# A two-layer hybrid decoder trunk on one NeuronCore: parameter rows fetched with one transfer per kind and turned one tile later, SBUF operands moved by 64 bytes, a table load and three convolution taps placed elsewhere

## What is computed

```python
def token_mixer(h, w_in, w_gate_up, b_gate, gla_norm_w, conv_w, conv_b, cn_w, cn_b, w_out):
    z = h @ w_in
    q, k, v, g, gr, ca, cb = split(z)
    gate_logit = gr @ w_gate_up + b_gate
    log_a = log_sigmoid(gate_logit) / 16
    o = rmsnorm(gla_chunked(q / 8, k, v, log_a), gla_norm_w) * silu(g)
    u = ca * sigmoid(cb)
    u = causal_dwconv(u, conv_w, conv_b)            # 31 taps, each channel by itself
    u = silu(layernorm(u, cn_w, cn_b))
    return concatenate([o, u]) @ w_out

for l in range(2):
    x = x + token_mixer(rmsnorm(x, ln1_w[l]), ...)
    h = rmsnorm(x, ln2_w[l])
    x = x + (swiglu(h, ...) if l == 0 else moe_swiglu(h, ...))
return rmsnorm(x, final_norm_w)
```

## Time and profile before

| | us |
|---|---|
| median of 3 runs | 1210.83 (1210.68 to 1210.93) |
| the profiled execution | 1211.27 |
| its span, first to last instruction | 1209.4 |
| PE busy in it | 1191.6 (99%) |
| DVE busy | 966.9 (80%) |
| ACT busy | 784.1 (65%) |

### The profile page before, as it was taken

The page is one execution under the profiler, slowest core; times in us unless marked ns, Lnnn a source line. Parts: engine busy times, 40 slices in busy tenths (PEclk is TensorE's granted clock), DMA queues, the critical chain, the costliest instruction groups (busy, mean ns, idle before and its releaser), DMA issues.

```text
span 1209.4 us, 16633 instructions
## 1 busy us (share of the span) xinstructions
PE 1191.6 (99%) x6712; PEld 1020.5 (84%) x6712; DVE 966.9 (80%) x890; ACT 784.1 (65%) x693; POOL 93.9 (8%) x160
## 2 busy tenths in 40 slices
PE   8999999999999999999999999999999999999997
PEld 7997999999899788888888888888888888888885
DVE  4988664445667879899979879879889879979987
ACT  5857644334565757677677768668668668767764
POOL 8320000000122000000000000000000000000000
PEclk9999999999999999999999999999999999999999
DMA  8982555555557259999999999999999999999980
GB/s 246 354 247 73 192 174 180 197 181 179 204 176 242 67 190 360 387 369 390 378 368 392 374 377 385 375 377 386 377 387 374 383 383 372 379 386 374 395 331 37
DMA packets 185003, 362.78 MB, mean 300 GB/s; under 512 B 10568, under 2 KB 70746, under 8 KB 184922
## 3 DMA queue, kind: packets, MB, share of 16 engines
q1 hardware_dynamic: 178170, 343.22, 79.4%
q0 software_dynamic: 6736, 18.43, 4.3%
q10 hardware_dynamic: 16, 0.00, 0.0%
HBM read 350.64 MB, written 7.86 MB: 296 GB/s over the span
## 4 chain that ended last, share of the span: by engine, by line
PE 93%; DVE 3%; ACT 1%; SPq 1%; issue 1%; DMA 0%; ACTq 0%; DVEq 0%
PE YB L2215 18%; PE WBS L2194 13%; PE WBS L2196 13%; PE WBS L2195 13%; PE YB L1804 5%; PE WBS L1731 5%; PE WBS L1733 4%; PE WBS L1732 4%; PE YB L2206 2%; PE WBS L1765 2%; PE YB L2230 2%; PE WBS L1767 2%; PE WBS L1766 2%; PE YB L1985 1%; PE YB L1785 1%; PE YB L1731 1%
## 5 line engine op out<-in xcount | busy, mean ns | idle before, releaser
L1006 DVE TENSOR_TENSOR w_lo<-raw,w_hi 128x2048 fp32r<-128x2048 f32 x319 | 716.1, 2285 | 85.8 <-ACT w_hi L611 85.6
L611 ACT ACTIVATE w_hi<-raw 128x2048 fp32r<-128x2048 f32 x324 | 598.3, 1914 | 12.8 <-DMA raw<-in_w_in 8.4
L2194 PE MATMUL WBS<-w_hi,t_hi 128*128 128x512 f32 x704 | 279.0, 396 | 0.5 <-DVE w_lo L1006 0.5
L2196 PE MATMUL WBS<-w_hi,t_lo 128*128 128x512 f32 x704 | 275.1, 391 | 0.0
L2195 PE MATMUL WBS<-w_lo,t_hi 128*128 128x512 f32 x704 | 274.2, 389 | 0.0
L2194 PEld LDWEIGHTS WBS<-w_hi,t_hi 128*128 128x128 f32 x704 | 132.2, 188 | 29.5 <-issue 2.5
L2196 PEld LDWEIGHTS WBS<-w_hi,t_lo 128*128 128x128 f32 x704 | 132.1, 188 | 28.5
L2195 PEld LDWEIGHTS WBS<-w_lo,t_hi 128*128 128x128 f32 x704 | 132.4, 188 | 26.3
L1731 PE MATMUL WBS<-t_hi,w_lo 128*128 128x256 f32 x448 | 127.5, 285 | 0.0
L1732 PE MATMUL WBS<-t_hi,w_hi 128*128 128x256 f32 x448 | 126.8, 283 | 0.0
L1733 PE MATMUL WBS<-t_lo,w_hi 128*128 128x256 f32 x448 | 126.7, 283 | 0.0
(11 more groups left out here) (320 smaller groups left out, 1390.9 us busy)
## 6 DMA issues: line engine op xcount, KB each, us to landing
raw<-in_we_down SPq DMA_DIRECT2D x88, 1024.0 KB, 7.1
raw<-in_we_gate SPq DMA_DIRECT2D x80, 1024.0 KB, 6.8
raw<-in_we_up SPq DMA_DIRECT2D x80, 1024.0 KB, 6.8
raw<-in_w_in SPq DMA_DIRECT2D x19, 1024.0 KB, 5.8
raw<-in_wd_gate SPq DMA_DIRECT2D x11, 1024.0 KB, 5.3
raw<-in_wd_up SPq DMA_DIRECT2D x11, 1024.0 KB, 5.3
raw<-in_wd_down SPq DMA_DIRECT2D x11, 1024.0 KB, 4.9
raw<-in_w_out SPq DMA_DIRECT2D x8, 1024.0 KB, 9.3
```

The costliest lines, as they stand in the source:

```text
L611: act.activation(w_hi[:, hi_slot(n, item), :], raw[slot][:], ACT.Copy).then_inc(hi_ready, 1)
L1006: dve.tensor_tensor(w_lo[slot][:], raw[slot][:], w_hi[:, hi_slot(n, item), :].bitcast(F32), ALU.subtract).then_inc(lo_ready, 1)
L2194: pe.matmul(bank, xs_hi[:, k0 + k, :], hi[:, k, :], start=start, stop=False)
L2196: ins = pe.matmul(bank, xs_lo[:, k0 + k, :], hi[:, k, :], start=False, stop=stop)
```

## The change

- **Transfers.** `small()` is called once. `conv_w`, `b_gate`, `conv_b`, `cn_w`, `cn_b` and `gla_norm_w` are each fetched for both layers with one transfer: 6 transfers in place of 12, of the same bytes in all. The rows of `pv_rows`, and so the columns of `pv`, now stand by kind and then by layer, and `param(l, at0, count, k)` gives a column's place.
- **Turning.** In layer 0 `turn_params()` follows tile 1 of V0 on PE, where it stood ahead of it. Both of its instructions wait for `rows_ready`, now for 7 transfers.
- **`ident4`.** DVE's reduction of the identity (L1219), which only the convolution weights need later, follows the copy of `gr_t`.
- **Addresses.** `idle` grows from 48 to 64 numbers. Every tile behind it moves up by 64 bytes: those that stood 64 bytes past a multiple of 128 now start on one, and a few (`shift_w`, `o_ss`, `rout`, `before`, `slot_no`) the other way round.
- **Table.** `preload(ACT.Sqrt)` stands ahead of `place(0)` in both layers.
- **Taps.** In layer 1 the last `conv(5)`, which stood ahead of `sum_groups(0)`, is cut: `conv(3)` now stands between `add_ahead(0)` and `head_sums(0)`, and `conv(2)` stays.

```diff
-        idle = sb("idle", [P, 48])
+        idle = sb("idle", [P, 64])
...
+        def param(l, at0, count, k=0):
+            return slice(L * at0 + count * l + k, L * at0 + count * l + k + 1)
...
-            def small(l):
-
-                sp.dma_start(tap_rows[2 * TAPS * l:2 * TAPS * (l + 1), :], conv_w[l, :, 0:2 * P].rearrange("w (c p) -> w c p", p=P)).then_inc(rows_ready, 16)
+            def small():
+
+                sp.dma_start(tap_rows[0:2 * TAPS * L, :], conv_w[:, :, 0:2 * P].rearrange("l w (c p) -> (l w) c p", p=P)).then_inc(rows_ready, 16)
                 for src, at0, k in ((b_gate, PV_BG, KT), (conv_b, PV_CB, CT), (cn_w, PV_CW, CT), (cn_b, PV_CBB, CT), (gla_norm_w, PV_GN, 1)):
-                    r = l * NPV + at0
-                    sp.dma_start(pv_rows[r:r + k, :], src[l].rearrange("(c p) -> c p", p=P)).then_inc(rows_ready, 16)
+                    sp.dma_start(pv_rows[L * at0:L * (at0 + k), :], src.rearrange("l (c p) -> (l c) p", p=P)).then_inc(rows_ready, 16)
...
-                        for layer in range(L):
-                            small(layer)
+                        small()
...
                     gates()
+                    preload(ACT.Sqrt)
                     place(0)
-                    preload(ACT.Sqrt)
                     head_squares()
...
                     dve.tensor_copy(taps[:].rearrange("p l w c -> p (l w c)"), YB[:, 2, 0:pv_at])
-                    dve.tensor_reduce(ident4[:], ident[:].rearrange("p (s j) -> p j s", s=4), AX, ALU.add).then_inc(ident4_ready, 1)
...
                 dve.tensor_copy(gr_t, YB[0:2 * RANK, 0, 0:T]).then_inc(gr_copied, 1)
+                if l == 0:
+                    dve.tensor_reduce(ident4[:], ident[:].rearrange("p (s j) -> p j s", s=4), AX, ALU.add).then_inc(ident4_ready, 1)
...
                     add_ahead(0)
+                    conv(3)
                     head_sums(0)
                     head_sums(1)
                     head_gates()
                     add_ahead(1)
                     head_lo(0)
                     head_lo(1)
-                    conv(5)
+                    conv(2)
                     sum_groups(0)
...
                 if l == 0:
+                    tokens_tile("V0", 1)
                     turn_params()
-                    tokens_tile("V0", 1)
...
-                pe.wait_ge(rows_ready, 16 * (6 * L + 1))
+                pe.wait_ge(rows_ready, 16 * 7)
```

More of the change, by code:

```diff
@@ L138, in trunk @@
         NPV = KT + 3 * CT + 1
-        pv = sb("pv", [P, L, NPV])
+        pv = sb("pv", [P, L * NPV])
         s_gr = ExitStack()
@@ L719, in head_hi @@
                         act.activation(t_hi[:, 2 * g:2 * g + 2, :].rearrange("p h t -> p (h t)"), WB[g], ACT.Copy,
-                                       scale=pv[:, l, PV_GN:PV_GN + 1]).then_inc(mix_hi, 1)
+                                       scale=pv[:, param(l, PV_GN, 1)]).then_inc(mix_hi, 1)
                 def place(i):
@@ L729, in place @@
                             act.activation(acc[rows, c, :], conv_bank(l, i)[64 * j:64 * j + 32, T * h_:T * (h_ + 1)], ACT.Identity,
-                                           bias=pv[rows, l, PV_CB + c:PV_CB + c + 1]).then_inc(conv_placed, 1)
+                                           bias=pv[rows, param(l, PV_CB, CT, c)]).then_inc(conv_placed, 1)
                 if l:
@@ L740, in mixer @@
                     act.activation(Difs[:, 0, k, :], YB[:, 1, T * k:T * (k + 1)], ACT.Abs,
-                                   bias=pv[:, l, PV_BG + k:PV_BG + k + 1]).then_inc(gate_abs, 1)
+                                   bias=pv[:, param(l, PV_BG, KT, k)]).then_inc(gate_abs, 1)
                 act.wait_ge(gate_abs, KT * (l + 1))
@@ L842, in mixer @@
                         act.activation(by_tile[t][:, c, :], acc[:, c, P * t:P * (t + 1)], ACT.Silu,
[L843 removed]
+                                       scale=pv[:, param(l, PV_CW, CT, c)], bias=pv[:, param(l, PV_CBB, CT, c)]).then_inc(c_silu, 1)
                     act.wait_ge(c_silu, CT * (TT * l + t + 1))
@@ L1125, in conv @@
                             dve.tensor_scalar(dst, cu[:, c, 0:T], taps[:, l, 0, c:c + 1],
-                                              pv[:, l, PV_CB + c:PV_CB + c + 1], ALU.mult, ALU.add).then_inc(conv_step[chain], 1)
+                                              pv[:, param(l, PV_CB, CT, c)], ALU.mult, ALU.add).then_inc(conv_step[chain], 1)
                         elif before_it == 0:
@@ L1193, in head_lo @@
                     dve.scalar_tensor_tensor(out=t_lo[:, 2 * g:2 * g + 2, :].rearrange("p h t -> p (h t)"),
-                                             in0=WB[g], scalar=pv[:, l, PV_GN:PV_GN + 1],
+                                             in0=WB[g], scalar=pv[:, param(l, PV_GN, 1)],
                                              in1=t_hi[:, 2 * g:2 * g + 2, :].rearrange("p h t -> p (h t)").bitcast(F32),
@@ L1223, in mixer @@
                                       ALU.mult).then_inc(router_ready, 1)
-                    dve.tensor_copy(pv[:].rearrange("p l c -> p (l c)"),
-                                    YB[:, 2, pv_at:pv_at + L * NPV]).then_inc(params_ready, 1)
+                    dve.tensor_copy(pv[:], YB[:, 2, pv_at:pv_at + L * NPV]).then_inc(params_ready, 1)
                 if l == 0:
@@ L1233, in mixer @@
                 for k in range(KT):
-                    ins = dve.tensor_scalar(cum[:, k, :], YB[:, 1, T * k:T * (k + 1)], pv[:, l, PV_BG + k:PV_BG + k + 1], 0.0,
+                    ins = dve.tensor_scalar(cum[:, k, :], YB[:, 1, T * k:T * (k + 1)], pv[:, param(l, PV_BG, KT, k)], 0.0,
                                             ALU.add, ALU.min)
```

## The result

| | before, us | after, us |
|---|---|---|
| median | 1210.76 (1209.12 to 1210.93, 4 runs) | 1202.45 (1202.36 to 1203.56, 4 runs) |
| the profiled execution | 1211.27 | 1202.36 |
| its span | 1209.4 | 1200.5 |

The change makes the kernel faster by 0.64%: the ratio is 0.9936, with a 95% interval from 0.9919 to 0.9954. The prediction had the sign right and the size wrong. It said 1204.9 us, with a range that ended at 1203.6, and the gain is 8.3 us, not 5.9.

What follows compares the result with a forecast made beforehand. PE work was taken to bound the kernel, so only PE's waits and slow clock would pay. Terms 4.53 + 1.4 gave 5.9 us, from the median 1210.83 to 1204.9 us; range 1203.6 to 1206.9.

Steps and rivals of the forecast that it cites:

- Addresses: I take 0: SBUF tile starts moved by 64 bytes: no gain counted, with 1 us of gain allowed for the range.
- The loss itself: Experts' and dense products slowed by the new tile starts: at 10 ns per product 1214.5 us; chance 0.02.
- Addresses pay: Rival: the new tile starts gain 1 us more, 1203.9 us, perhaps 1203.5; chance 0.06.
- The late unit 2: At CB0 in layer 0: PE would wait 0.55 us if unit 2's load stayed where it was.
- The prediction's first rival: Merging doesn't shorten SP's issue, so CB0 waits 0.55 us for unit 2: 1205.5 to 1206.0 us; chance 0.08.
- Rows and clock: Start of layer 0 on PE: parameter-row wait of 2.83 us and slow clock of 1.70 us vanish, gain 4.53 us.
- Merging moves SP's queue up: SP's queue: six fewer transfers bring everything behind up to 3.04 us earlier; 2.7 us taken.
- Layer 1: End of layer 1's attention: `head_sums` 0.31 us earlier, turned heads to `w_out` 1.15 us shorter; together taken as 1.4.
- Table, layer 0: Moved table load in layer 0: gains 0, as the chain there has no step of ACT between.
- Nothing later gave the time back: Behind layer 1's mixer, instructions and distances to PE stay and PE waits for no transfer, so no gain is lost.

Runs made afterwards that it cites:

- a_all64: Changed kernel with 64 bytes of padding in front of the first tile, so every SBUF tile moves up together: 1202.6 us, ratio 0.9932.
- a_eT128b: Changed kernel with 128 bytes of padding ahead of `eT_hi`, moving `eT_hi` and `eT_lo` (small tiles behind also by 128): 1207.8 us, ratio 0.9976.
- a_eT192: Changed kernel with `eT_hi` and `eT_lo` moved up by 192 bytes, tiles behind by 256: 1204.4 us, ratio 0.994.
- a_eT256: Changed kernel with `eT_hi` and `eT_lo` moved up by 256 bytes, tiles behind also by 256: 1202.4 us, ratio 0.9922.
- a_eT32b: Changed kernel with `eT_hi` and `eT_lo` moved up by 32 bytes, small tiles behind by 128: 1208.0 us, ratio 0.9976.
- a_eT64: Changed kernel with `eT_hi` and `eT_lo` moved up by 64 bytes, small tiles behind by 128: 1208.4 us, ratio 0.9979.
- b_turn: Kernel before with only `turn_params()` moved behind tile 1 of V0, all twelve transfers kept: 1208.9 us, ratio 0.9989.
- a_tabback: Changed kernel with the table load put back behind `place(0)` in both layers: 1202.5 us, ratio 0.9932.
- a_taps5: Changed kernel with layer 1's five taps together again, ahead of the sums over blocks: 1203.4 us, ratio 0.9941.
- b_idle64: Kernel before with only `idle` grown to 64 numbers, the address edit alone: 1207.3 us, ratio 0.9968.
- a_turnback: Changed kernel with `turn_params` ahead of tile 1 of V0 again, merged transfers kept: 1203.4 us, ratio 0.9942.

## Why the prediction was wrong, and where it was right

**The step that failed is "Addresses: I take 0".** It put 395 ns for a tile 64 bytes past a multiple of 128 beside 396 for one on a multiple, the means of two different groups, and took the likeness as proof. The trace of before already had the difference. By its median the group with `t_hi` takes 389 ns, where that with `eT_hi` takes 394 (388/394/475 above):

```profile
L2194 PE MATMUL WBS<-w_hi,t_hi x704: 387/389/486, 443.8 to 1188.8; 128*128 128x512 f32 x176
```

49 of these 704 products take over 440 ns, against 9 of the 320 with `eT_hi`, and pull the mean up to 396. In all these kernels as built, `t_hi` starts at the place of `w_hi` within 256 bytes, and 389 ns is also the median that `eT_hi` reaches there. What makes the 49 long is open. Within the one group, the loaded operand's place is worth up to 7 ns of a mean of 392. The variable was wrong as well. It is not the multiple of 128 (a_all64, a_eT128b), but the place within 256 bytes relative to other tiles (a_eT192 against a_eT256 shows it cleanly; a_eT32b, a_eT64 and a_eT128b with the tiles behind moved as well). That the partner is the streamed operand `w` is argued, not shown: it is read at the same time, and the best place is the one where both starts agree, but `raw`, `w_lo`, `t_hi`, `t_lo` and others start at that place too.

**The range failed with it, and by its own working.** For a loss the prediction let the products cost 10 ns each, 9.6 us in all. For a gain it allowed 1 us, by counting only the 18 us in which PE is not busy. Nothing excluded that PE's products themselves get faster, and that is where it came: 2.3 us over the 960 products of L2215 and 96 more that load the same tiles, some 2 ns each. The same 10 ns as a gain reach down to 1195.3, well past 1202.45. The loss itself stood outside the stated range, at a chance of 0.02, and the rival "Addresses pay", at 0.06, had the sign right, but the wrong engine and less than half of the 2.5 us. The chances of the forecast and its rivals add up to 1.00, so the 0.1 for what could not be named is in none of them.

The 16-byte lines of the Trainium skill, page "SBUF — State Buffer", section "Specifications (TRN2)", on which the prediction leaned, can't tell these placements apart, since 32, 64, 128 and 192 bytes all start a line; the runs differ by 6 us. The same page says in its section "Who interferes with whom" that PE reads the streamed operand and the weights through two independent ports and waits on nobody. By that rule the place of the loaded tile would be free; here products whose loaded tile stands 64 bytes past the best place take 1.5% longer (398 ns in place of 392), and the measurement decides.

**A second size was wrong and did not show.** The late unit 2 was priced at 0.55 us, and another 0.5 for what it passes down. b_turn shows 2.5 (4.6 less 2.1). The prediction's first rival, with merging that doesn't help, would have been at about 1207.3 and not at 1205.5 to 1206.0.

**What held.**
- Rows and clock: 4.53 us predicted, 4.6 measured; logits predicted at 22.70, at 22.21 with the start 0.4 earlier.
- Merging moves SP's queue up: 2.7 us were taken of at most 3.04. The first unit behind the rows is issued 3.65 us earlier, 0.6 of it because the whole queue began earlier in this execution, which leaves 3.04. Doubled rows cost the queue next to nothing: 0.83 us for 124 rows, where the first transfer of before took 0.82 for 62.
- Layer 1: 0.31 and 1.15 us predicted, 0.3 and 1.1 measured. a_tabback takes 0.2 of the first away, a_taps5 nearly all of the second (12.95 us again). The way from the turned heads to `w_out` is 11.91 us in both layers, as predicted.
- Table, layer 0: nothing, as predicted (a_tabback).
- Nothing later gave the time back.

## What to carry to other kernels

When a change moves SBUF tiles, give the address term the same bound in both directions, per product and times all the products that read a moved tile, and look for the effect within one group of instructions across two layouts. Between two groups of one layout compare shortest and median too, never the means alone: a few long products hid 5 ns here. A tile that PE loads thousands of times is worth a try at other offsets within 256 bytes: one padding tile, one run. When a wait is removed by doing other work first, look at what is queued behind the same transfers; here it would have taken back about half of the gain without the merging.

## What the runs showed of the hardware that was not expected

- The start of PE's loaded operand relative to the other tiles, within 256 bytes, sets the time of a product of 128 x 512 that streams beside the loads: 392 ns at the best place, 395 at 64 bytes short, 397 to 399 at 32, 64 or 128 past (the last three with the tiles behind moved by 128 bytes too). From one start to the next that is 227 ns on average, 229 at 64 short and 233 at 64 past. Moving by 256 bytes reproduces the group's shortest, median and longest duration (389, 389, 478 ns) exactly, and so does moving all tiles by 64.
- Such an effect is in none of the waits and hardly in the busy share, which is 99% of the span before and after. The mean and the median of a group and the distance from its first to its last instruction show it.
- PE's granted clock fell to 0.50 behind an idle stretch of 2.83 us (before). It stayed at 1.00 behind one of 2.0 us (b_idle64) and one of 0.6 us (a_turnback), with the same work around them.
